# A two-block transformer kernel on one core: the first stage in another order, two modulation pieces summed by TensorE, and products that nobody reads

## The reference

```python
cond = silu(c)
mod = cond @ w_ada + b_ada                    # six parts of 2048: sh1, sc1, g1, sh2, sc2, g2
h = x * (1.0 + sc1) + sh1
z = h @ w_in + b_in                           # 2048 x 9216
y_a = spatial_gating(gelu(z_u), gelu(z_v), ...) @ w_branch_a
y_b = hyena(z_h, ..., hyena_filters(...)) @ w_branch_b
```

## Time and profile before

| | |
|---|---|
| median of 3 runs | 2645.43 us (2644.23 to 2646.96) |
| the profiled execution's own time | 2642.59 us |
| its span | 2641.3 us |
| PE busy | 2599.3 us, 98% |
| DVE busy | 1846.0 us, 70% |
| ACT busy | 1290.1 us, 49% |
| mean granted clock of TensorE | 0.995 |

### The profile page before, as it was taken

How to read it: one execution, slowest core, us unless ns; L and a number is a source line. 1 busy time by engine, 2 the same in 40 slices (tenths; PEclk the granted TensorE clock), 3 DMA queues, 4 the chain that set the end, 5 groups by cost and what they waited for, 6 DMA issues and landing times.

```text
span 2641.3 us, 31620 instructions
## 1 busy us (share of the span) xinstructions
PE 2599.3 (98%) x12546; PEld 2172.6 (82%) x12546; DVE 1846.0 (70%) x1927; ACT 1290.1 (49%) x1566; POOL 32.1 (1%) x55
## 2 busy tenths in 40 slices
PE   7899999999999999999999999999999999999999
PEld 3689988878888888888888888888888888988887
DVE  7879899988876644577776767755554665656565
ACT  2345544444444444555555544444444654555463
POOL 0000000000000000000000000000000000000000
PEclk9899999999999999999999999999999999999999
DMA  8998878798788755665656555555656556634554
GB/s 346 360 376 321 299 274 320 261 318 327 271 270 276 262 190 180 198 208 196 194 191 205 180 189 185 183 191 191 210 186 196 182 191 168 176 126 158 195 176 143
DMA packets 276584, 598.65 MB, mean 227 GB/s; under 512 B 21264, under 2 KB 46288, under 8 KB 260064
## 3 DMA queue, kind: packets, MB, share of 16 engines
q1 hardware_dynamic: 268272, 566.52, 63.1%
q0 software_dynamic: 4560, 21.56, 2.5%
q10 hardware_dynamic: 3616, 8.68, 0.9%
HBM read 586.24 MB, written 10.49 MB: 226 GB/s over the span
## 4 chain that ended last, share of the span: by engine, by line
PE 92%; DVE 5%; ACT 1%; DMA 1%; issue 1%; ACTq 0%; SPq 0%; DVEq 0%
PE ps L925 26%; PE ps L927 26%; PE ps L926 26%; PE ps L1050 2%; PE ps L1034 2%; PE ps L1036 2%; PE ps L1037 2%; DVE w_lo L2238 1%; DVE group_acc L2357 1%; DMA raw<-in_w_in 1%; PE ps L1433 1%; PE ps L1434 1%; PE ps L1435 1%; PE ps L1092 1%; PE ps L1085 0%
## 5 line engine op out<-in xcount | busy, mean ns | idle before, releaser
L2238 DVE TENSOR_TENSOR w_lo<-raw,w_hi 128x1024 fp32r<-128x1024 f32 x870 | 1050.3, 1221 | 673.2 <-ACT w_hi L1579 671.4
L1579 ACT CAST w_hi<-raw 128x1024 fp32r<-128x1024 f32 x870 | 906.6, 1051 | 1050.0 <-PE ps L927 913.3
L925 PE MATMUL ps<-w_lo,x_hi 128*128 128x512 f32 x2592 | 1021.2, 394 | 4.3 <-DVE w_lo L2238 2.8
L927 PE MATMUL ps<-w_hi,x_lo 128*128 128x512 f32 x2592 | 1011.6, 390 | 0.0
L926 PE MATMUL ps<-w_hi,x_hi 128*128 128x512 f32 x2592 | 1011.1, 390 | 0.0
L925 PEld LDWEIGHTS ps<-w_lo,x_hi 128*128 128x128 f32 x2592 | 488.3, 188 | 107.8 <-DVE w_lo L2238 4.6
L927 PEld LDWEIGHTS ps<-w_hi,x_lo 128*128 128x128 f32 x2592 | 488.1, 188 | 102.9
L926 PEld LDWEIGHTS ps<-w_hi,x_hi 128*128 128x128 f32 x2592 | 488.7, 189 | 100.3 <-issue 1.4
L2266 DVE SCALAR_TENSOR_TENSOR ada_acc<-raw,cond,ada_acc 128x2048 f32<-128x2048 f32 x64 | 150.1, 2345 | 2.0 <-DMA raw<-in_w_ada 1.0
L925 PE MATMUL ps<-w_lo,pooled_hi 128*128 128x512 f32 x384 | 150.2, 391 | 0.0
L927 PE MATMUL ps<-w_hi,pooled_lo 128*128 128x512 f32 x384 | 149.5, 389 | 0.0
(11 more groups left out here) (379 smaller groups left out, 2136.6 us busy)
## 6 DMA issues: line engine op xcount, KB each, us to landing
raw<-in_w_m SPq DMA_DIRECT2D x128, 1024.0 KB, 5.3
raw<-in_w_ada SPq DMA_DIRECT2D x64, 1024.0 KB, 5.7
raw<-in_pool_w_in SPq DMA_DIRECT2D x64, 1024.0 KB, 5.4
raw<-in_w_in SPq DMA_DIRECT2D x56, 1024.0 KB, 7.5
raw<-in_k_mod SPq DMA_DIRECT2D x32, 1024.0 KB, 6.6
raw<-in_pool_w_out SPq DMA_DIRECT2D x32, 1024.0 KB, 5.0
raw<-in_ple_w_gate SPq DMA_DIRECT2D x32, 1024.0 KB, 5.1
raw<-in_mla_w_in SPq DMA_DIRECT2D x24, 1024.0 KB, 5.1
```

Of the source, the lines that this page charges most:

```text
L925: mm(bank, xh, wl, start=start, stop=False)
L927: ins = mm(bank, xl, wh, start=False, stop=stop)
L1579: nc.scalar.copy(by_ktile(st, w_hi[st.half_slot(j, half)][:, 0:n]), raw_half(st, j, half)).then_inc(hi_split, 1)
L2238: tt(by_ktile(st, w_lo[slot][:, 0:n]), raw_half(st, j, half), by_ktile(st, w_hi[slot][:, 0:n].bitcast(F32)), ALU.subtract).then_inc(lo_spl ...
```

## The change

1. Before the second hidden layer TensorE makes 7 products, and after it 5, into a bank that nobody reads (`unread`).
2. Of groups 1 and 2 one modulation piece each, (1,2) and (2,6), is no longer added by VectorE. TensorE takes it straight from `raw`, in 16 products of one column with `cond` (`raw_block`), which stand between the products of unit (0,0) and of the second half of unit (1,1). They start the accumulation that `group_sum` ends. Its load is a "p" in `STREAM`; the slot is freed by `raw_summed`.
3. TensorE's order: `group_sum(1)` comes before `filter_product(3, 0)` and its spectrum, these and the units (0,2), (1,0), (1,1) take turns. Banks of the spectra and of the sum change with it.
4. VectorE's order: `filter_part(2, 1)` comes before the piece (1,4), `filter_part(3, 0)` and `filter_part(3, 1)` come later, group 2's scale comes before the split of w(2,0).
5. ScalarE's order: w(0,1) is rounded before spectrum (2,0) is copied, w(0,2) before (2,1); three of the four spectrum stores are issued during the stage, one is left at its end. The first two gelus move behind the first unit of `in_h`; VectorE's third output and the add behind it move there too.

```diff
-    ("first", 1, [("ggggggggw", ""), ("ggwggwggggw", ""), ("ggwggwggggw", ""), ("ggwggwgwgwgg", "wwww")]),
+    ("first", 1, [("ggggggggw", ""), ("ggwpgwggggw", ""), ("ggwggwggpgw", ""), ("ggwggwgwgwgg", "wwww")]),
...
+RAW_PIECE = (None, 2, 6, None)
...
     def spec_bank(it, m):
-        return 6 if it > 1 else 2 * m if it else 4 + 2 * m
+        return (2 * m, 4 + 2 * m, 2 + 2 * m, 6)[it]
 
     def sum_bank(q):
-        return 6 if q else 4
+        return 6 if q else 0
...
+                used_p = st.freed("p", i, j)
...
+                if used_p > 0:
+                    sync.wait_ge(raw_summed, used_p)
...
+        def unread(n):
+            for _ in range(n):
+                mm(ps[:, 5, 0:S], hid_pack[:, 0:P], feats, start=True, stop=True)
+
         pe.wait_ge(hidden_in, 16)
         mm(ps[0:HID, 0, 0:S], w1[0:EMB, :], feats[0:EMB, :], start=True, stop=True).then_inc(hid_mm, 1)
+        unread(7)
 
         pe.wait_ge(hid_sin, 1)
         mm(ps[:, 0, 0:S], w2[0:HID, :], hid_arg[0:HID, :], start=True, stop=True).then_inc(hid_mm, 1)
+        unread(5)
...
+        def raw_block(q, e, n):
+
+            st, u = ST["first"], RAW_PIECE[q]
+            j = group_ada(q, u)
+            col = e * 2 * CH + n * P
+            if e + n == 0:
+                pe.wait_ge(raw_full[st.slot(j)], st.landed(0, j))
+            ins = mm(ps[:, sum_bank(q), n:n + 1], raw[st.slot(j)][:, col:col + P], cond[:, 2 * u + e:2 * u + e + 1],
+                     start=e + n == 0, stop=False, skip_group_check=True)
+            if e == 1 and n == 7:
+                ins.then_inc(raw_summed, 1)
...
         pe.wait_ge(spec_copied, 4)
-        group_unit(0, 0)
+        for half in range(2):
+            group_half(0, 0, half, between=lambda n: raw_block(1, half, n))
         filter_product(2, 1)
+        pe.wait_ge(spec_copied, 5)
         group_half(0, 1, 0)
         spectrum(2, 1)
         group_half(0, 1, 1)
+        group_sum(1)
+
+        pe.wait_ge(spec_copied, 6)
+        group_half(0, 2, 0)
+        pe.wait_ge(mod_group, 2)
         filter_product(3, 0)
+        group_half(0, 2, 1)
         spectrum(3, 0)
-        group_sum(1)
-
-        group_unit(0, 2)
-        group_unit(1, 0)
+        group_half(1, 0, 0)
         filter_product(3, 1)
+        group_half(1, 0, 1)
+        spectrum(3, 1)
         group_half(1, 1, 0)
-        spectrum(3, 1)
-        group_half(1, 1, 1)
+        pe.wait_ge(spec_copied, 8)
+        group_half(1, 1, 1, between=lambda n: (raw_block(2, 0, n), raw_block(2, 1, n)))
         group_sum(2)
...
         group_hi(0, 1)
+        group_round(0, 1)
         spectrum_out(2, 0)
-        group_round(0, 1)
+        group_round(0, 2)
         spectrum_out(2, 1)
-        group_round(0, 2)
-        spectrum_out(3, 0)
+        spectrum_store(0)
         group_round(1, 0)
...
         group_round(1, 1)
+        spectrum_out(3, 0)
+        spectrum_store(1)
         group_round(1, 2)
         spectrum_out(3, 1)
+        spectrum_store(2)
         group_round(2, 0)
...
         def vu_end():
-            spectrum_store(0)
-            spectrum_store(1)
+            spectrum_store(3)
             columns_load()
-            gelu(0)
-            gelu(1)
...
-        for i in range(2):
-            run(st, i, sgu_std)
+        run_at(st, 0, {2: lambda: (gelu(0), gelu(1)), 4: lambda: sgu_std(0, 0), 12: lambda: sgu_std(0, 1)})
+        run(st, 1, sgu_std)
...
-        add_first(1, 2)
+        add_first(1, 3)
         filter_part(2, 1)
-        add_first(1, 3)
-        add_first(1, 4)
         group_rest(0, 2)
-        add_first(1, 5)
-        filter_part(3, 0)
-        add_first(1, 6)
-        add_first(1, 7)
+        for u in range(4, 8):
+            add_first(1, u)
         group_rest(1, 0)
...
+        filter_part(3, 0)
         add_first(2, 1)
         group_rest(1, 1)
         add_first(2, 2)
+        group_rest(1, 2)
         filter_part(3, 1)
-        add_first(2, 3)
-        group_rest(1, 2)
-        for u in range(4, 8):
+        for u in (3, 4, 5, 7):
             add_first(2, u)
+
+        group_scale(2)
         group_rest(2, 0)
```

More of the change, by code:

```diff
@@ L417, in block_kernel @@
     group_added = sem("group_added")
+    raw_summed = sem("raw_summed")
     ident_in = sem("ident_in")
@@ L549, in group_ada, with added_by @@
     def group_ada(q, u):
-        return nth_load("g", 8 * q + u)
+        return [j for j, of in enumerate(ST["first"].pattern) if of != "w"][8 * q + u]
+    def added_by(q, u):
+        return sum(n != RAW_PIECE[p] for p in range(q + 1) for n in range(u if p == q else 8))
     def first_half(q, c, half):
@@ L910, in _, with products @@
         mm = nc.tensor.matmul
-        def products(st, i, j, half, kt, hi, lo, banks, first, last, tiles=(0, 1)):
+        def products(st, i, j, half, kt, hi, lo, banks, first, last, tiles=(0, 1), between=None):
             slot = st.half_slot(j, half)
@@ L925, in products @@
                     mm(bank, xh, wl, start=start, stop=False)
+                    if between:
+                        between(4 * c + 2 * t)
                     mm(bank, xh, wh, start=False, stop=False)
+                    if between:
+                        between(4 * c + 2 * t + 1)
                     ins = mm(bank, xl, wh, start=False, stop=stop)
@@ L1080, in filter_product @@
             if it > 1:
[L1081 removed]
+                pe.wait_ge(spec_copied, (2, 3, 4, 7)[2 * it + d - 4])
             for t in range(2):
@@ L1094, in spectrum, with group_half @@
             ins.then_inc(spec_mm, 1)
+        def raw_block(q, e, n):
[8 more added lines that the diff above has]
+                ins.then_inc(raw_summed, 1)
         def group_sum(q):
             if q == 0:
-                pe.wait_ge(spec_copied, 2)
-            elif q < 3:
-                pe.wait_ge(spec_copied, 6 + q)
-            else:
+                pe.wait_ge(spec_copied, 1)
+            elif q == 3:
                 pe.wait_ge(part_kept, 1)
-            pe.wait_ge(group_added, 8 * (q + 1))
+            whole = RAW_PIECE[q] is None
+            pe.wait_ge(group_added, added_by(q, 8))
             for n in range(8):
                 ins = mm(ps[:, sum_bank(q), n:n + 1], group_acc[q % 2][:, n * P:(n + 1) * P], ones[:, 0:1],
-                         start=True, stop=True)
+                         start=whole, stop=True, skip_group_check=not whole)
             ins.then_inc(group_summed, 1)
         st = ST["first"]
-        def group_half(q, c, half, first=None, last=None):
+        def group_half(q, c, half, first=None, last=None, between=None):
             pe.wait_ge(fm_lo if half else h_lo, q + 1)
             products(st, 0, group_weights(q, c), half, 4 * q + 2 * half, x_hi, x_lo, pair(c),
-                     q == 0 and half == 0 if first is None else first, q == 3 and half == 1 if last is None else last)
+                     q == 0 and half == 0 if first is None else first, q == 3 and half == 1 if last is None else last,
+                     between=between)
         def group_unit(q, c, first=None, last=None):
@@ L2346, in add_first @@
             if u:
-                dve.wait_ge(group_added, 8 * q + u)
+                dve.wait_ge(group_added, added_by(q, u))
             elif q >= 2:
@@ L2500, in _, with vu_third @@
         vu_out(1)
-        add_ada(st, 0, 2, 2, 1)
-        vu_out(2)
+        def vu_third():
+            vu_out(2)
+            add_ada(ST["in_vu"], 0, 2, 2, 1)
         def moments(src, width, t):
@@ L2525, in sgu_scaled @@
             tt(v, v, sgu_b[:], ALU.add).then_inc(vn_ready, 1)
-        run_at(ST["in_h"], 0, {4: lambda: vu_out(3), 6: lambda: split_dft(0), 8: sgu_norm, 12: lambda: conv_sides(0)}, lambda i, n: (2, 2 + n))
+        run_at(ST["in_h"], 0, {2: vu_third, 4: lambda: vu_out(3), 6: lambda: split_dft(0), 8: sgu_norm, 12: lambda: conv_sides(0)}, lambda i, n: (2, 2 + n))
         run_at(ST["in_h"], 1, {0: lambda: sgu_scaled(0), 4: lambda: conv_sides(1), 6: lambda: split_dft(2), 8: lambda: sgu_scaled(1),
```

6 lines of the change are left out of this document (1 added, 5 removed).

## The result

| | before | after |
|---|---|---|
| median, 19 runs each | 2645.43 us (2639.48 to 2647.38) | 2651.27 us (2646.1 to 2653.45) |
| ratio after to before | | 1.0021, 95% interval 1.0015 to 1.0028 |
| profiled execution, own time / span | 2642.59 / 2641.3 us | 2650.23 / 2648.9 us |
| PE busy | 2599.3 us | 2616.1 us |
| DVE busy | 1846.0 us | 1840.4 us |

The forecast was 2641.9 us, the range ended at 2648.0. The change costs 5.8 us in the medians, 7.6 us in the two profiled executions.

The account below looks back on a forecast made before the run. TensorE's waits in the first 180 us were taken as the bound, with VectorE and DMA engines nearly full. Gains of 2.2 us to sum 3 and 1.3 into in_h made 3.5: 2641.9 us, range 2635.5 to 2648.0.

Parts of the forecast that it names:

- The filter unit with 16 blocks: Unit (0,0) on TensorE: 16 one-column blocks at 0.23 us each add 3.6 us to its 5.5.
- the lower bound: Blocks on TensorE: half of 3.6 us, if only one of a block's two weight loads shows.
- The window's wait: VectorE's filter window (2,1) waits 5.8 us for a product behind unit (0,0), then runs 57.8 to 59.0.
- The seam: Passage into in_h: 1.3 of TensorE's 1.6 us wait gained by moving gelus and VectorE's third output.
- The stores' 1.2 us: Three spectrum stores moved into 65 to 100 us: 1.2 us charged to loads that matter, bounds 0 and 9.9.
- rival C: Stores push the loads issued from 65 to 105 us, price 9.9 us: 2651.1 us; chance 0.09.
- signs of being wrong: 16 blocks adding well under 3 or over 5 us, loads at 65 to 105 us landing over 8 us after issue, new TensorE waits after 180.
- sum 1 at the full clock: TensorE from sum 1's end at 73.6: filter work takes 17.7 us to 91.3; sum 2 at 109, full clock.
- rival B: No clock gained: unread products do not raise it, or the 5.2 us wait before sum 1 drops it; 2644.9 us; chance 0.16.
- the adds taken off VectorE: Two adds of one piece, 2.65 us, leave VectorE; group sum 1 at 71.8, not 75.40, 3.6 us gained, 1.6 from the start.
- Nothing after 180 changes: After 180 us: no change; the moved ada add leaves unit 3's load 1.4 us of slack.
- The start: Unread products raise TensorE's clock: first scale at 40.0 instead of 41.6, 1.6 us gained; bounds 0.3 lost, 1.7 gained.

Follow-up runs that it names:

- run 3: The changed kernel with all 32 pieces added by VectorE and no blocks on TensorE, the rest kept; ratio 0.9999 to the kernel before.
- run 2: The changed kernel with its four spectrum stores at their old places, the rest kept; ratio 1.0017 to the kernel before.
- run 12: The changed kernel with all pieces added by VectorE, window (3,1) ahead of the split of w(1,2), and spectrum stores at their old places; ratio 0.9993 to the kernel before.
- run 16: The kernel before with three spectrum stores moved early, nothing else; ratio 1.0003 to the kernel before.
- run 17: The changed kernel with 11 more products that nobody reads in the wait before sum 1; ratio 1.0007 to the kernel before.
- run 15: The changed kernel with only its new order left: no blocks, no unread products, stores and seam as before; ratio 1.0003 to the kernel before.

## Why the prediction was wrong

**Right.** The filter unit with 16 blocks: first product 47.64, next filter product 57.16, 9.5 us, where run 3 took 52.10 - 46.23 = 5.9; 3.65 us for 16 blocks against the 3.6 forecast. The Trainium skill (TensorE: Matmul & The Clock Gate, the table at its head) says that weight loads are pulled ahead of matmuls in flight. Between wide products a block still cost the 0.23 us that it costs in a group sum, so the lower bound, which that sentence would have put nearer, did not come. The window's wait was 6.12 for 5.8, sum 1 came 32.1 behind scale 0, as forecast (71.8 - 40.0 = 31.8). The seam: from sum 3 to in_h's first product 32.85 before and 31.25 now, 1.6 for 1.3. The stores' 1.2 us: runs 2, 12 and 16 give 1.1, -1.1 and 0.8, none of which can be told from 0 or from 1.2. The Trainium skill (DMA: Bandwidth & Descriptors, Issuing engines are not separate DMA queues) says that transfers started by different engines run on the same 16 engines and interleave; the landings above agree (8.9 against 7.0 us).

**Right by its number only: rival C.** It gave 2651.1 us, and 2651.27 were measured. One of the signs of being wrong that I had named came too: the loads issued from 65 to 105 us land 8.8 us after their issue in the median, over the 8 of the sign. The kernel before has 6.7 there; the 5.0 us that I took for a load issued at 97 are its median of 38 to 60 us.

```profile
DMA to landing us min/median/max: 4.8/8.8/10.3
```

But C puts 9.9 us on the stores, and taking them back gives 1.1 (at most 4). That its number was met is chance.

**The step that failed: "sum 1 at the full clock".** The forecast had sum 1 end at 73.6, the filter work and four half units follow in 17.7 us, then "sum 2 starts 0.5 us later than before, but at the full clock". The 5.3 us wait dropped the clock: sum 1 took 3.57 us, and from its end at 76.8 to the end of the fourth half unit, whose slot ScalarE rounds into at 97.51, it took 20.7 us, not 17.7 (the first half unit alone 5.27 us, the other three 3.1 to 3.2). TensorE went on at 101.00 for the forecast 94.8; the 3.53 us of waiting before it were forecast at 3.5, but behind them the spectrum ran at the half clock as well, 2.7 us more. Counted from scale 0, sum 2 was forecast at 69.0 and came at 75.1: 0.3 us were late at sum 1, 4.7 come from sum 1 to the end of the fourth half unit, 2.7 from the spectrum and the half unit behind it, 0.3 from the half unit with blocks, and 1.9 came back, since the load of (2,6) no longer had to be waited for. This is rival B's mechanism, which I priced at 3 us with a chance of 0.16; run 17, which takes away only the fall at sum 1, gives 3.7.

I had both sides in the rows, a spectrum at full speed after 3.64 us of idling and a sum at half speed after 7.90, and took the kind side for 5.2. In all 15 traces with 5.3 to 6.5 us of waiting before sum 1 it takes 3.57 or 3.58 us. And the kind side was not so kind: in the trace of the kernel before the clock fell after all, behind that wait and the 1.61 us before sum 1, 3.3 us after this sum began, for seven products of 0.63 us in place of 0.39:

```profile
78.69 0.63 PE L925 MATMUL ps<-w_lo,x_hi 128*128 128x512 f32 x1
...
82.04 0.39 PE L927 MATMUL ps<-w_hi,x_lo 128*128 128x512 f32 x1
```

**The step that hid the loss: the blocks in the sum.** Their terms were right, and so was sum 1, but the gain that I read from it, "the adds taken off VectorE", was not theirs. Against the same order without them (run 15, or run 3) the first piece's 2.65 us off VectorE gain nothing: VectorE's window waits for the very unit that the blocks lengthen, all of it is given back, and sum 1 is 3.5 us later. Together the two pieces cost 5.8 us, which is the whole loss against the kernel before; I compared each step with that kernel, where the order's 5.2 us at sum 1 covered it.

**Behind sum 2.** Forecast: 35.4 us from sum 2 to sum 3; measured 37.6. TensorE waits 1.03 and 0.56 us for splits and 0.64 for the last add, 1.2 more than forecast; the splits wait for ScalarE's roundings, and these 3.7 to 5.4 us each for a load. The other 1.0 us I cannot place. **"Nothing after 180 changes"** was wrong by one wait: 0.94 us before in_h's third unit (197.74; the expectations call it the fourth), 0.9 to 1.2 in every run with the new seam. It is not the slot of the moved add. VectorE works without a wait from 176.68 to 193.9, with the third output and that add behind the first split; ScalarE waits 6.52 us for the fourth output to apply a gelu to it, and the rounding of the third unit stands behind this gelu:

```profile
193.91 1.06 ACT L1767 ACTIVATE vu<-vu 128x1024 f32<-128x1024 f32 x1 [6.52 <-DVE vu L2494]
```

So the seam's 1.6 us shrink: 1.9 us on the kernel before with an interval that takes in 0, 0.3 on the change.

**The start** gained what I forecast in half of the executions only: the scale of group 0 began at 39.6 to 39.8 in 7 of the 15 traces with unread products and at 41.2 to 41.5 in 8. Without them (five traces) it was 41.2 to 42.7. Taking them out costs 1.1 us of median, inside the interval.

What stays open: runs 3, 15 and 16 have sum 3 of their traces 3.2, 3.3 and 5.3 us later than before, but medians 0.3 us under and twice 0.8 over it; one profiled execution (in these 20 it lies from 3.0 us under to 3.3 us over the median of its kernel) is no measure of a part that small. In run 16 a part of it is the clock: its spectrum behind the 3.64 us wait took 6.77 us, not 3.70. How the 5.8 us split between the two pieces is known only to about 2 us.
